# Sparse attention in a hybrid decoder block: values as 128 weight columns per key head, both heads in one PSUM region

## What is computed

```python
def block(inp):                      # one tile of 128 query tokens, for each of 2 key heads with 3 query heads (g) each
    ...
    s = einsum('bhgqd,bhkd->bhgqk', q_b, k_g) * scale
    p_s = masked_softmax(s, ...)                       # over chosen blocks of all earlier keys
    o_s = einsum('bhgqk,bhqkd->bhgqd', p_s, v_g)
    ...
    p_w = masked_softmax(s, (diff >= 0) & (diff < WINDOW))   # over the last 512 keys
    o_w = einsum('bhgqk,bhkd->bhgqd', p_w, v_b)
    return g_b[..., 0:1] * o_c + g_b[..., 1:2] * o_s + g_b[..., 2:3] * o_w
```

## Time and profile before

| what | us |
|---|---|
| median of 3 runs (lowest, highest) | 1063.14 (1062.17, 1066.04) |
| span of the profiled execution | 1063.3 |
| PE busy, DVE busy, ACT busy, POOL busy | 1025.7, 813.6, 635.0, 501.6 |
| stage with the value products, 245 to 531 us: PE busy | 280.1 of 286.0 |

### The profile page before, as it was taken

The page is one execution under the profiler, slowest core; times in us unless marked ns, Lnnn a source line. Parts: engine busy times, 40 slices in busy tenths (PEclk is TensorE's granted clock), DMA queues, the critical chain, the costliest instruction groups (busy, mean ns, idle before and its releaser), DMA issues.

```text
span 1063.3 us, 19006 instructions
## 1 busy us (share of the span) xinstructions
PE 1025.7 (96%) x7090; PEld 833.7 (78%) x7090; DVE 813.6 (77%) x1140; ACT 635.0 (60%) x1201; POOL 501.6 (47%) x653
## 2 busy tenths in 40 slices
PE   4999999998999999999999999999999998999997
PEld 4978878986777778777688787888887786888885
DVE  5798895755667886877577598899899999656755
ACT  6634423347777766777865454666666667546443
POOL 2356424725453654542320277788788886000000
PEclk9999999996999999999999999999999999999999
DMA  9245311352122122112263612233443335955961
GB/s 276 68 119 178 110 57 27 70 125 58 41 60 59 27 53 49 29 30 60 80 209 136 198 53 80 79 119 122 127 127 123 123 115 192 382 178 180 334 239 79
DMA packets 159522, 126.77 MB, mean 119 GB/s; under 512 B 63908, under 2 KB 137928, under 8 KB 159432
## 3 DMA queue, kind: packets, MB, share of 16 engines
q1 hardware_dynamic: 157992, 120.32, 37.7%
q10 hardware_dynamic: 1440, 5.24, 1.2%
HBM read 99.79 MB, written 25.71 MB: 118 GB/s over the span
## 4 chain that ended last, share of the span: by engine, by line
PE 60%; DVE 7%; POOL 4%; ACT 3%; issue 3%; DMA 0%; DVEq 0%; ACTq 0%; POOLq 0%
PE psum L2475 14%; PE psum L2263 12%; PE psum L1771 5%; PE psum L1720 5%; PE psum L1704 4%; POOL slab_q L2087 4%; PE psum L1546 4%; PE psum L1689 3%; PE psum L1886 3%; PE psum L2269 2%; DVE arena L2171 1%; DVE arena L2165 1%; PE psum L1625 1%; PE psum L1605 1%; ACT arena L1219 1%
## 5 line engine op out<-in xcount | busy, mean ns | idle before, releaser
L2087 POOL TENSOR_TENSOR slab_q<-arena,slab_p 128x512 fp32r<-128x512 f32 x127 | 208.2, 1667 | 45.5 <-ACT slab_p L2080 45.4
L2475 PE MATMUL psum<-dn_p,ap_p 128*128 128x512 f32 x352 | 110.2, 392 | 2.7 <-DVE arena L2171 1.4
L2475 PE MATMUL psum<-dn_q,ap_q 128*128 128x512 f32 x352 | 109.7, 391 | 0.0
L2263 PE MATMUL psum<-t_p,slab_p 128*128 128x512 f32 x272 | 106.3, 391 | 1.3 <-ACT arena L2144 0.8
L2263 PE MATMUL psum<-t_q,slab_q 128*128 128x512 f32 x272 | 105.9, 389 | 0.0
L2080 ACT ACTIVATE slab_p<-arena 128x512 fp32r<-128x512 f32 x127 | 78.2, 627 | 38.7 <-PE psum L2263 13.9
L2301 DVE TENSOR_TENSOR dn_q<-arena,dn_p 128x1024 fp32r<-128x1024 f32 x41 | 50.2, 1224 | 56.3 <-ACT dn_p L2291 56.0
L1431 DVE CUSTOM_DVE_ANT_0 psum<-psum,arena 128x640 f32<-128x640 f32 (+7 forms) x96 | 67.7, 718 | 31.2 <-PE psum L1689 30.6
L2291 ACT ACTIVATE dn_p<-arena 128x1024 fp32r<-128x1024 f32 x44 | 46.6, 1058 | 70.0 <-PE psum L2475 63.6
L3051 PE MATMUL psum<-h_p,cm_p 128*128 128x512 f32 (+1 forms) x288 | 87.5, 375 | 0.6 <-DVE arena L2958 0.6
L3051 PE MATMUL psum<-h_q,cm_q 128*128 128x512 f32 (+1 forms) x288 | 86.9, 373 | 0.0
(11 more groups left out here) (319 smaller groups left out, 2636.4 us busy)
## 6 DMA issues: line engine op xcount, KB each, us to landing
arena<-in_ffn_w_up SPq DMA_DIRECT2D x44, 512.0 KB, 4.9
arena<-in_ffn_w_down SPq DMA_DIRECT2D x44, 512.0 KB, 3.9
arena<-in_w_in SPq DMA_DIRECT2D x20, 512.0 KB, 3.9
act_mid<-arena SPq DMA_DIRECT2D x18, 512.0 KB, 2.6
arena<-act_mid SPq DMA_DIRECT2D x36, 256.0 KB, 4.7
arena<-in_x SPq DMA_DIRECT2D x16, 512.0 KB, 4.6
qkv_mid<-arena ACTq DMA_DIRECT2D x9, 512.0 KB
arena<-qkv_mid SPq DMA_DIRECT2D x8, 576.0 KB, 4.9
```

The lines of the kernel that those rows point to most:

```text
L2087: pool.tensor_tensor(slab_q[n % RING], part_source(i, j), slab_p[n % RING], ALU.subtract).then_inc(late("up_lo")[0], 1)
L2263: ins = pe.matmul(mult_ps(i, j), w[:, k], x[:, k], start=k == 0 and x is x_p[i] and i in (1, 2, 5), stop=True, skip_group_check=True)
L2475: ins = pe.matmul(dn_ps[t % HT][:, n * 512:(n + 1) * 512], x[:, tok], w[:, n * 512:(n + 1) * 512], start=first and x is ap_p[s], stop=True ...
```

## The change

The values are stored with 128 columns per key head: the own head's 64 values stand in the own half of the columns, the other half is zero. With such weights one product of 384 moving columns (3 heads x 128 tokens) on the whole array writes all 128 partitions of bank 7: key head 0 on partitions 0 to 63, key head 1 on 64 to 127. The two key heads of a kind add up in the same region (`start` is set only for the first block of key head 0), and one copy of 128x384 per tile and kind brings both to `ot`. The zero halves are filled once by four memsets on POOL. The array of values doubles; the second half lies behind the arena, and the space set aside for descriptors of dynamic DMAs is made smaller for it. The order `MIX` is not changed.

```diff
-        val = R.view(36960, [NT, 2, KV * HD])
+        val = [R.view(36960, [NT, KV, P]), plain("val_window", ARENA, [NT, KV, P])]

+        def kinds_before(t, kind):
+            return GROUPS.index((t, kind, 0)) // KV

             def Nu(t, kind, kv):
-                rows = (LO, HI)[kv]
-                act.wait_ge(sem("n_om"), GROUPS.index((t, kind, kv)) + 1)
-                for tok in (LO, HI):
-                    act.activation(ot[rows, :, tok], psum[tok, 7, 0:GDIM // 2].rearrange("p (g c) -> p g c", g=GRP), ACT.Copy)\
-                        .then_inc(late("n_ou")[0], 1)
+                if kv:
+                    act.wait_ge(sem("n_om"), kinds_before(t, kind) + 1)
+                    act.activation(ot.rearrange("p g c -> p (g c)"), psum[:, 7, 0:GDIM], ACT.Copy).then_inc(late("n_ou")[0], 1)

# NV(t, kind, kv, b)
-                if b == k0:
-                    if (kind, kv) == (0, 0):
-                        pe.wait_ge(sem("n_ot"), t + 1)
-                    elif n:
-                        pe.wait_ge(*late("n_ou", 2 * n))
-                for tok in (LO, HI):
-                    ins = pe.matmul(psum[tok, 7, 0:GDIM // 2], val[:, b, kind, HD * kv:HD * (kv + 1)], pt[x % 2][:, :, tok],
-                                    start=b == k0, stop=True, skip_group_check=True)
-                if b == k1 - 1:
+                first = (kv, b) == (0, k0)
+                if first and kind == 0:
+                    pe.wait_ge(sem("n_ot"), t + 1)
+                elif first and t:
+                    pe.wait_ge(*late("n_ou", kinds_before(t, kind)))
+                elif first:
+                    pe.wait_ge(sem("val_zero"), 2 * KV)
+                ins = pe.matmul(psum[:, 7, 0:GDIM], val[kind][:, b, kv], pt[x % 2].rearrange("p g c -> p (g c)"),
+                                start=first, stop=True, skip_group_check=True)
+                if (kv, b) == (KV - 1, k1 - 1):
                     ins.then_inc(sem("n_om"), 1)

# POOL, before the rotation of the keys
+            pool.wait_ge(sem("cm_done"), U_KC)
+            for kind in range(2):
+                for kv in range(KV):
+                    pool.memset(val[kind][:, :, kv, HD * (1 - kv):HD * (2 - kv)], 0.0).then_inc(sem("val_zero"), 1)

# ACT, once per tile of 128 tokens
-                act.activation(val[:, t], tm_bank("KV", t).rearrange("p (w c) -> p w c", w=4)[:, 1:4:2, :], ACT.Copy,
-                               scale=1.0 / SPLIT_W).then_inc(sem("tm_act"), 1)
+                for kind in range(2):
+                    own_half = val[kind][:, t].rearrange("p k c -> p (k c)").rearrange("p (k c) -> p k c", c=HD)[:, 0:4:3]
+                    ins = act.activation(own_half, tm_bank("KV", t)[:, P * (2 * kind + 1):P * (2 * kind + 2)].rearrange("p (k d) -> p k d", k=KV),
+                                         ACT.Copy, scale=1.0 / SPLIT_W)
+                ins.then_inc(sem("tm_act"), 1)

-    nc = bacc.Bacc("TRN2", target_bir_lowering=False, num_devices=1)
+    nc = bacc.Bacc("TRN2", target_bir_lowering=False, num_devices=1, dynamic_dma_scratch_size=1024)
```

More of the change, by code:

```diff
@@ L86 @@
 TAPS = (0, 5, 4, 4) + 9 * (2,) + (5, 6, 6)
+ARENA = 53200
 class Regions:
@@ L430, in build @@
         arena_at = -(-nc.sbuf_base // 32) * 32
-        arena = ctx.enter_context(nc.sbuf_tensor("arena", [P, 53200], F32))
+        arena = ctx.enter_context(nc.sbuf_tensor("arena", [P, ARENA], F32))
         R = Regions(arena)
@@ L1671, in Nc3 @@
                     pe.wait_ge(sem("vcbd_in"), 32)
-                pe.wait_ge(*late("n_ou", 2 * (4 * t + 2)))
+                pe.wait_ge(*late("n_ou", kinds_before(t, 1) + 1))
                 for p in range(3):
@@ L1710, in NV @@
                 x = nsa_nt.index(("NT", t, kind, kv, b))
-                n = GROUPS.index((t, kind, kv))
                 k0, k1 = key_blocks(t, kind)
-                if b == k0:
-                    if (kind, kv) == (0, 0):
-                        pe.wait_ge(sem("n_ot"), t + 1)
-                    elif n:
-                        pe.wait_ge(*late("n_ou", 2 * n))
-                for tok in (LO, HI):
-                    ins = pe.matmul(psum[tok, 7, 0:GDIM // 2], val[:, b, kind, HD * kv:HD * (kv + 1)], pt[x % 2][:, :, tok],
-                                    start=b == k0, stop=True, skip_group_check=True)
-                if b == k1 - 1:
+                first = (kv, b) == (0, k0)
[8 more added lines that the diff above has]
+                if (kv, b) == (KV - 1, k1 - 1):
                     ins.then_inc(sem("n_om"), 1)
@@ L1726, in Nb @@
                 pt_free(("Nb", t, kind))
-                pe.wait_ge(*late("n_ou", 2 * (GROUPS.index((t, kind, 1)) + 1)))
+                pe.wait_ge(*late("n_ou", kinds_before(t, kind) + 1))
                 for g in range(GRP):
```

## The result

The changed kernel takes 1081.3 us (median of 4 runs, 1080.74 to 1082.19) against 1063.33 (1062.17 to 1066.04) before: 1.0165 times as long, interval 1.015 to 1.018. It is slower by 18.0 us; the forecast was 1086 with a range of 1078 to 1093. The direction and the price of the columns were right; the sum was 4.7 us too high.

A forecast was written before the change was run, and what follows sets the result against it. The prediction took PE, which runs its list in order almost without stopping, as the bound. Columns +42.4 and switches -16.4 gave +26.0; less 3 for waits, +23: 1063.3 + 23 = 1086 us, range 1078 to 1093.

The forecast's parts named there:

- The columns: Value products on PE: a step costs 0.646 us against 0.325, at 0.84 ns per column; 132 steps add 42.4 us.
- Rival (a): Value products on PE: full-array records stream a column per cycle, so the kernel gets faster, 1049 us; 3 in 100.
- The switches: Switches of the array's division around value-product runs: 62 entries save 0.14 us each, 77 exits 0.10; -16.4 us.
- Waits that vanish: PE's own waits in the value-product stage shrink with ACT's relief and longer steps: 3 us, bounds nothing and 5.9.
- the two signs: Wrong if the distance in a step is far from 0.32, or PE's idle time in the stage exceeds what the page shows.
- Rival (b): PE has more room than its waits show; half of the 26 us is absorbed: 1076 us; 6 in 100.
- The filling: POOL's four memsets (2.2 us) hide before its first rotation; ACT's two-piece copies, bounds 0 and 1.4 us, taken as 0.
- The lower clock: About 240 to 257 us at 1.2 GHz: three or so runs there cost +0.6 us more; taken as 0.
- The base: The sum starts from the profiled span of 1063.3 us, said to agree with the median 1063.14 within 0.2 us.
- likeliest case: Whole-kernel time of 1080 to 1092 us, from 1083.4 and 1091.3 with 3 us for rounding; 85 in 100.
- Rival (d): Time sits in terms left at nothing: filling +2.2 + 1.4, lower clock +0.6, unshrunk waits +3; 1093.5 at most; no chance given.
- Rival (c): Full-array load not hidden under a stream at value-product steps: up to 14.5 us, 1100, half of it 1093; 6 in 100.

The follow-up runs named there:

- experiment 1: The changed kernel with each value product streaming only the first 192 of its 384 columns: 1052.04 us, 0.9886 of the kernel before.
- experiment 2: The changed kernel with each value product cut into two calls of 192 columns: 1082.21 us, 1.017 of the kernel before.
- experiment 9: The changed kernel with each value product made twice into the same sum: 1166.26 us, 1.0962 of the kernel before.
- experiment 7: The changed kernel with the one copy out per tile and kind cut into four of 64x192: 1086.04 us, 1.0204 of the kernel before.
- experiment 8: The kernel before without the upper token half's copy out from the second tile on, 9.0 us less on ACT: 1063.41 us, ratio 0.9995.
- experiment 4: The kernel before with ACT copying values in two pieces and four POOL memsets into unused memory: 1065.09 us, ratio 1.0008.
- experiment 10: The kernel before with one more 384-column product ahead of each of the first tile's four value products: 1064.6 us, ratio 1.0006.

## Why the prediction was right, and where it was off

**The columns** (+42.4): right. 0.323 us per record, 0.646 per step, shown in the trace of after and by experiments 1, 2 and 9. The rate was read from records of at most 192 columns and held at 384. Rival (a), a column per cycle, is refuted. By the Trainium skill, TensorE: Matmul & The Clock Gate, section Back-to-back issue gap, N/2.4 + 2.5 ns gives an estimate of 162.5 ns for 384 columns; 322 to 323 ns was measured for a plain float32 record, and the measurement decides.

**The switches** (-16.4): nearly right. Entries and exits between full-array lines are gone as priced. Wrong was that the 29 entries from a 64 by 64 step only keep their cost. The load of the second record after a switch is only partly covered, and it is now one of 128 columns. After, the second record of such a run starts 427 ns behind the first in place of 323; before, the second pair started 207 ns behind the first in place of 162. A run of one entered so takes 0.749 us in place of 0.648, 0.10 more, where a load of 64 columns cost 0.05. 29 x 0.05 = 1.45 us more. With this the work is +27.2, forecast +26.0.

**Waits that vanish** (-3, bounds 0 and 5.9): mis-sized, and this is the larger part of the miss. 5 to 10.5 us vanished, at or beyond the upper bound, which I had taken from the page's idle time. That is the flaw in the step: idle time on PE leaves out what hides under a matmul's tail. It is one of the two signs that the prediction itself had named for being wrong. Rival (b) named this and gave it half of the work; in all 9.2 of 27.2 us didn't arrive, the clock's share included, about a third. Which wait gave how much stays open. Experiment 7 shows that four copies in the place of the single one cost 4 to 5 us in the kernel after, and experiment 8 that freeing ACT without more is worth at most 1.6 us in the kernel before.

**The filling** (0): right, by the trace of experiment 4 and POOL's remaining 2.47 us.

**The lower clock** (0, at most +0.6): the wrong sign. I treated the 17 us near 240 as given and asked what a longer step would cost in it. The longer step shortened the stretch itself, to between 3 and 7 us. The head gave back 2.8 us, and some of what the rest gave back may be the clock's too; by the 56 executions some 2.6 us in all go with it. That more streaming raised the granted clock here is shown by experiment 10; its worth in time rests on the spread of before's executions, since experiment 10's own time didn't fall, and isn't shown.

**The base.** I said that the profiled span and the median agree within 0.2 us. In every run whose span and time are both recorded, the time is 1.7 to 2.0 us above the span (after: 1080.4 and 1082.19). So the profiled execution of before took about 1065 us, 2 above its median. It didn't matter for the sum's terms, which are differences, but a span should not be set equal to a time.

Together: +1.2 for the loads, -3.7 for what vanished in the rest of the mixer and -2.8 for its head lead from +23 to +17.7; 18.0 was measured.

**The range.** 1081.3 lies within it, near the bottom of the likeliest case. Two of its sums don't come out as written. Rival (d) adds up to 1086 + 2.2 + 1.4 + 0.6 + 3 = 1093.2, not 1093.5, and either is just outside the range, not inside. The likeliest case takes its 3 us for rounding at the bottom (1083.4 to 1080) and not at the top, where it would give 1094.3.

**Rival (c)**, a full-array load that isn't hidden: refuted by experiment 2, which doubles these loads for 0.9 us. It is true only behind a switch of the array's division.

## What to carry to other kernels

Before padding an operand with zeros to fill the array, ask whether the pieces already run side by side: here two column halves did, at 0.325 us for both, and one padded product for both takes 0.646. That is 0.32 us more at each of 132 steps, while the switches had cost 0.24 at each of 91 runs. Price PE work by distances between starts and find waits by comparing these with an undisturbed stream; idle time leaves out what hides under a matmul's tail. And an order that looks wasteful may cover latencies: grouping the products saved 5.7 us in their own distances and lost 14.5 in the other lines.

## What the runs showed of the hardware

- Granted clock: with four more 384-column products in a partly idle stretch the median granted clock of an execution rose from 0.991 to 0.996, and the time at 1.2 GHz in that stretch was 3.4 us, against 10 to 24 in traces with before's first tile. Work added to PE there can give back part of its own cost: 2.6 us more work cost no more than 2.0 us (1.0006, up to 1.0019).
- Two calls of 192 columns cost 0.9 us more over 132 steps than one call of 384 each: an additional record and its load of 128 columns hide under 0.16 us of streaming.
- Behind a switch of the array's division a load shows: the second record (before, the second pair) starts 0.05 us late with loads of 64 columns and 0.10 with loads of 128.
- Two plain float32 records on different column halves overlap fully: dropping one of each two leaves a run at 0.47 us and the kernel's ratio at 1.0006.
